# Gate/up products of the feed-forwards: 19 of 22 pieces as seven block products of half the tokens, modulation products moved behind them

## What is computed

```python
for l in range(DEPTH_2):            # 2
    mod = (c_act @ w_mod[l] + b_mod[l]).reshape(c.shape[0], N_MOD, D_MODEL)
    h = modulate(x, g_norm[l, 0], mod[:, 0], mod[:, 1])
    x = x + 0.5 * mod[:, 2][:, None, :] * swiglu_2(h, w_ffn1_gu[l], w_ffn1_down[l])
    ...
    h = modulate(x, g_norm[l, 2], mod[:, 6], mod[:, 7])
    x = x + 0.5 * mod[:, 8][:, None, :] * swiglu_2(h, w_ffn2_gu[l], w_ffn2_down[l])

def modulate(x, g, shift, scale):
    return rmsnorm_2(x, g) * (1.0 + scale[:, None, :]) + shift[:, None, :]
```

## Time and profile before

| | us |
|---|---|
| median of 3 runs | 3005.95 |
| lowest, highest | 3005.54, 3012.29 |
| span of the profiled execution | 2999.2 |
| TensorE busy in it | 2885.2 |
| VectorE, ScalarE, POOL busy in it | 1808.9, 1307.9, 326.0 |

### The profile page before, as it was taken

The page is one execution under the profiler, slowest core; times in us unless marked ns, Lnnn a source line. Parts: engine busy times, 40 slices in busy tenths (PEclk is TensorE's granted clock), DMA queues, the critical chain, the costliest instruction groups (busy, mean ns, idle before and its releaser), DMA issues. The chain is left out here.

```text
span 2999.2 us, 39355 instructions
## 1 busy us (share of the span) xinstructions
PE 2885.2 (96%) x13800; PEld 2294.2 (76%) x13800; DVE 1808.9 (60%) x2177; ACT 1307.9 (44%) x1512; POOL 326.0 (11%) x425
## 2 busy tenths in 40 slices
PE   8999798999999999999999999999999999999998
PEld 4876566777777778888877788887888877788886
DVE  7747857999999987555158555425554156533323
ACT  5125535888888863233136322213322136332312
POOL 0100012333333320000000000000000000000000
PEclk9989999999999999999999999999999999999999
DMA  8552236999999996553222255423554222122221
GB/s 320 169 197 92 100 152 247 370 361 372 373 365 355 367 367 237 192 188 134 98 102 71 94 200 195 154 95 106 193 194 154 98 96 77 65 104 98 97 87 68
DMA packets 115843, 555.50 MB, mean 185 GB/s; under 512 B 20656, under 2 KB 22192, under 8 KB 73776
## 3 DMA queue, kind: packets, MB, share of 16 engines
q1 hardware_dynamic: 89264, 491.43, 44.3%
q0 software_dynamic: 26496, 62.96, 5.9%
HBM read 549.10 MB, written 37.75 MB: 196 GB/s over the span
## 5 line engine op out<-in xcount | busy, mean ns | idle before, releaser
L168 ACT ACTIVATE stream_high<-stream_raw 128x2048 fp32r<-128x2048 f32 x151 | 289.3, 1917 | 799.8 <-PE ffn_ps_psum L470 755.0
L173 DVE TENSOR_TENSOR stream_low<-stream_raw,stream_high 128x2048 fp32r<-128x2048 f32 x156 | 356.7, 2287 | 406.9 <-ACT stream_high L168 406.5
L468 PE MATMUL ffn_ps_psum<-h_high_f,stream_high 128*128 128x512 f32 x1344 | 523.3, 389 | 0.2 <-DVE stream_low L173 0.2
L470 PE MATMUL ffn_ps_psum<-h_high_f,stream_low 128*128 128x512 f32 x1344 | 522.8, 389 | 0.0
L469 PE MATMUL ffn_ps_psum<-h_low_f,stream_high 128*128 128x512 f32 x1344 | 522.8, 389 | 0.0
L312 DVE TENSOR_TENSOR expert_low<-expert_raw,expert_high 128x2048 fp32r<-128x2048 f32 x128 | 292.8, 2288 | 6.1 <-ACT expert_high L308 2.5
L692 DVE TENSOR_TENSOR ffn_sg<-ffn_sg,ffn_ps_psum 128x512 f32<-128x512 f32 x88 | 60.5, 687 | 388.5 <-PE ffn_ps_psum L470 385.6
L468 PEld LDWEIGHTS ffn_ps_psum<-h_high_f,stream_high 128*128 128x128 f32 x1344 | 252.3, 188 | 53.5 <-DVE stream_low L173 0.6
L469 PEld LDWEIGHTS ffn_ps_psum<-h_low_f,stream_high 128*128 128x128 f32 x1344 | 252.3, 188 | 52.8 <-issue 0.2
L470 PEld LDWEIGHTS ffn_ps_psum<-h_high_f,stream_low 128*128 128x128 f32 x1344 | 252.3, 188 | 51.8
L468 PE MATMUL ffn_ps_psum<-ffn_hid_high,stream_high 128*128 (+1 forms) x704 | 277.6, 394 | 3.2 <-DVE ffn_sg L692 3.2
(11 more groups left out here) (497 smaller groups left out, 5050.7 us busy)
## 6 DMA issues: line engine op xcount, KB each, us to landing
expert_raw<-in_exp_gu SPq DMA_DIRECT2D x128, 1024.0 KB
stream_raw<-in_ffn_gu SPq DMA_DIRECT2D x88, 1024.0 KB, 5.0
expert_raw<-in_exp_dn SPq DMA_DIRECT2D x64, 1024.0 KB
con<-in_w_mod SPq DMA_DIRECT2D x120, 512.0 KB
stream_raw<-in_ffn_dn SPq DMA_DIRECT2D x44, 1024.0 KB, 5.0
mix_mod_rows<-in_w_ada POOLq DMA_DIRECT2D x32, 512.0 KB
stream_raw<-in_w_in SPq DMA_DIRECT2D x16, 1024.0 KB, 5.0
pieces_raw<-in_w_in SPq DMA_DIRECT2D x11, 1024.0 KB, 6.9
```

Of the source, the lines that this page charges most:

```text
L168: self.nc.scalar.activation(self.high[:, q], self.raw[:, q], ACT.Copy).then_inc(self.high_done, 1)
L173: self.nc.vector.tensor_tensor(self.low[:, q], self.raw[:, q], self.high[:, q].bitcast(F32), ALU.subtract)\
L468: mm(out, w[0], x[0], start=start, stop=False)
L470: return mm(out, w[1], x[0], start=False, stop=stop)
```

## The change

**Products.** Pieces 0 to 2 of the up phase stay as they were (`PLAIN` = 3). For pieces 3 to 21 the gate and up weights are one 2 by 2 matrix of blocks: gate or up, times the first or last four of the 8 width blocks (the host stores the four quarters one behind the other, `PLACE`). The tokens are 2 by 2 too: first or last four width blocks, times the first or last 256 tokens. Two by two block matrices can be multiplied with seven block products in place of eight (Winograd's form of Strassen's), from sums of blocks on both sides and sums of the products. A product is 4 width blocks × 3 matmuls of 256 columns, so a piece is 84 matmuls of 256 columns, where it was 48 of 512.

**Sums of the tokens**, once per feed-forward: the normed tokens in 32 bits on ScalarE (8 Identity), 4 sums of 1024 on VectorE, and high and low parts of them (`t_high`, `t_low`).

**Sums of the weights**, for each of the 19 pieces: products one, two and four take three quarters of the weights as they are, whose high part (1536 columns) ScalarE puts in `pure_high` and whose low part VectorE puts in `pure_low`. Then VectorE makes four sums of 512 columns in place in `stream_raw`, each of the last three waiting for the one before, and the split of before (2048 columns, ScalarE then VectorE) is made of those sums, for the products six, seven, five and three. ScalarE's waits for all four sums.

**Sums of the products.** ScalarE keeps product one and five (256 columns each), VectorE adds: first rows (2 × 256), middle rows (512), last rows (512 and 256); ScalarE makes silu of the gate, VectorE the product of gate and up into `hid`, in 32 bits. The parts of `hid` are no longer made per piece: POOL makes the high part of two tiles (`window`) and VectorE the low part, per piece of the down phase, in the space of the pure blocks.

**Moved.** The modulation rounds stand in the down phase, 4 products per piece, behind the split and the window; their loads stand between the down loads on SP. The late norm's squares go to ScalarE's turns of pieces 8 to 11, its sums to POOL, its 8 products to rounds 1 and 2 of the down phase. Its sum is TensorE's after piece 12, in bank 7.

The diff, cut to its core:

```diff
+PLAIN = 3
+LATE = 8
+PLACE = {(0, 0): 0, (0, 1): 1, (1, 1): 2, (1, 0): 3}
...
+plain_banks = [(0, 1), (6, 7), (0, 1)]
+half_bank = lambda s, i: ps[:, 6, TOK[s]] if i == two else ps[:, 3 * s + i // 2, TOK[i % 2]]
...
+        in_pairs(sp, FT, up, first=1)
+        down(0, 0)
+        down(0, 1)
         if beside:
-            def beside_up(g):
-                up(2 * g + 1, 0)
-                mod.load(sp, g, (0, 1))
-                up(2 * g + 1, 1)
-                mod.load(sp, g, (2, 3))
-                up(2 * g + 2, 0)
-                mod.load(sp, g, (4, 5))
-                up(2 * g + 2, 1)
+            def round_(g):
+                down(g + 1, 0)
+                mod.load(sp, g, (2, 3, 4, 5))
+                down(g + 1, 1)
                 mod.load(sp, g, (6, 7))
-            with sp.Fori(0, rounds) as g:
-                beside_up(g)
-        in_pairs(sp, FT, up, first=1 + 2 * rounds)
-        in_pairs(sp, HALF, down)
+                mod.load(sp, g + 1, (0, 1))
+            mod.load(sp, 0, (0, 1))
+            with sp.Fori(0, rounds - 1) as g:
+                round_(g)
+            down(rounds, 0)
+            mod.load(sp, rounds - 1, (2, 3, 4, 5, 6, 7))
...
+        def product(out, weights, place, x, tok, rows_=0, start=True, stop=True):
+
+            for k in range(4):
+                c = slice(place * S + k * P, place * S + (k + 1) * P)
+                mm = mm3(out, (weights[0][:, c], weights[1][:, c]), (x[0][:, rows_ + k, tok], x[1][:, rows_ + k, tok]),
+                         start=start and k == 0, stop=stop and k == 3)
+            return mm
+
+        def seven_products(r, s):
+            n = 2 * r + s
+            m = number(n)
+            pure, sums, t_ = (pure_h[:, s], pure_l[:, s]), (w.high[:, w.slot(s)], w.low[:, w.slot(s)]), (t_high, t_low)
+            tok0, tok1 = TOK
+            out = lambda i: half_bank(s, i)
+            pe.wait_ge(pure_low, m + 1)
+            pe.wait_ge(hid_done, n - 1)
+            product(out(one), pure, 0, h, tok0).then_inc(products, 1)
+            if not (isinstance(m, int) and m < 1):
+                pe.wait_ge(rows_made, 4 * m - 2)
+            product(out(two), pure, 1, h, tok0, 4).then_inc(products, 1)
+            if isinstance(n, int) and n == PLAIN:
+                pe.wait_ge(t_ready, 2)
+            product(out(four), pure, 2, t_, tok0, 4).then_inc(products, 1)
+            w.ready(pe, r, s)
+            pe.wait_ge(kept, 2 * m + 1)
+            product(out(six), sums, 0, t_, tok1, 4).then_inc(products, 1)
+            product(out(seventh), sums, 3, t_, tok1, 0).then_inc(products, 1)
+            product(out(five), sums, 2, t_, tok0, 0).then_inc(products, 1)
+            product(out(three), sums, 1, h, tok1, 4).then_inc(w.used, 1)
...
+        def silus(r, s):
+            m = number(2 * r + s)
+            act.wait_ge(rows_made, 4 * m + 4)
+            a(rows[s][:, 0:2, :], rows[s][:, 0:2, :], ACT.Silu).then_inc(silu_done, 1)
+
+        def keep_first(r, s):
+            m = number(2 * r + s)
+            act.wait_ge(products, 6 * m + 1)
+            if not (isinstance(m, int) and m < 2):
+                act.wait_ge(hid_done, 2 * r + (s - 1))
+            a(rows[s][:, 0, :], half_bank(s, one), ACT.Copy).then_inc(kept, 1)
+
+        def keep_fifth(r, s):
+            act.wait_ge(products, 6 * number(2 * r + s) + 6)
+            a(fifth[s], half_bank(s, five), ACT.Copy).then_inc(kept, 1)
+
+        def split_pure(r, s):
+            m = number(2 * r + s)
+            wait_loaded(act, r, s)
+            if not (isinstance(m, int) and m < 2):
+                act.wait_ge(products, 6 * m - 9)
+            a(pure_h[:, s], w.raw[:, w.slot(s), 0:3 * S], ACT.Copy).then_inc(pure_high, 1)
+
+        def split_sums(r, s):
             n = 2 * r + s
-            act.wait_ge(gate_ps, n + 1)
-            act.wait_ge(hid_low_done, n + 1)
-            nc.scalar.activation(sg[:, s, :], ps[:, 2 * s, :], ACT.Silu).then_inc(silu_done, 1)
+            act.wait_ge(sums_made, 4 * number(n) + 4)
+            act.wait_ge(w.used, n + (w.base - 1))
+            a(w.high[:, w.slot(s)], w.raw[:, w.slot(s)], ACT.Copy).then_inc(w.high_done, 1)
...
+        def body(r, s, silu=None, pure=True):
+            before = (r, 0) if s else (r - 1, 1)
+            behind = (r, 1) if s == 0 else (r + 1, 0)
+            (silu or silus)(*before)
+            keep_first(r, s)
+            split_sums(*behind)
+            keep_fifth(r, s)
+            if pure:
+                split_pure(r + 1, s)
...
+        def window(r, s):
+            n = 2 * r + s
+            pool.wait_ge(hid_done, 4 * r + 2 * s + 2)
+            if isinstance(n, int) and n < 2:
+                pool.wait_ge(products, 6 * number(FT - 2 + n) + 3)
+            else:
+                pool.wait_ge(w.used, n + (w.base + FT - 1))
...
+        def split_pure(r, s):
+            m = number(2 * r + s)
+            dve.wait_ge(pure_high, m + 1)
+            v.tensor_tensor(pure_l[:, s], w.raw[:, w.slot(s), 0:3 * S], pure_h[:, s].bitcast(F32), ALU.subtract).then_inc(pure_low, 1)
+        def make_sums(r, s):
+            m = number(2 * r + s)
+            a11, a12, a22, a21 = (w.raw[:, w.slot(s), i * S:(i + 1) * S] for i in range(4))
+            dve.wait_ge(pure_low, m + 1)
+            for i, (out, x, y, op) in enumerate(((a22, a21, a22, ALU.add), (a21, a11, a21, ALU.subtract),
+                                                 (a11, a22, a11, ALU.subtract), (a12, a12, a11, ALU.subtract))):
+                if i:
+                    dve.wait_ge(sums_made, 4 * m + i)
+                v.tensor_tensor(out, x, y, op).then_inc(sums_made, 1)
+        def first_rows(r, s):
+            m = number(2 * r + s)
+            q, made = rows[s], rows_made
+            dve.wait_ge(kept, 2 * m + 1)
+            dve.wait_ge(products, 6 * m + 4)
+            v.tensor_tensor(q[:, 2, :], q[:, 0, :], half_bank(s, six), ALU.add).then_inc(made, 1)
+            dve.wait_ge(made, 4 * m + 1)
+            v.tensor_tensor(q[:, 0, :], q[:, 0, :], half_bank(s, two), ALU.add).then_inc(made, 1)
+        def middle_rows(r, s):
+            m = number(2 * r + s)
+            q = rows[s]
+            dve.wait_ge(kept, 2 * m + 2)
+            v.tensor_tensor(q[:, 1:4:2, :], q[:, 2, :].unsqueeze(1).broadcast_to([P, 2, S // 2]), both_halves(s, five), ALU.add)\
+                .then_inc(rows_made, 1)
+        def last_rows(r, s):
+            n = 2 * r + s
+            q = rows[s]
+            dve.wait_ge(w.used, n + (w.base + 1))
+            dve.wait_ge(rows_made, 4 * number(n) + 3)
+            v.tensor_tensor(q[:, 1:3, :], q[:, 1:4:2, :], both_halves(s, three), ALU.add).then_inc(rows_made, 1)
+            dve.wait_ge(kept, 2 * number(n) + 2)
+            dve.wait_ge(rows_made, 4 * number(n) + 4)
+            v.tensor_tensor(q[:, 3, :], q[:, 3, :], fifth[s], ALU.add).then_inc(last_row, 1)
...
+            v.tensor_tensor(hid_tile(n).rearrange("p (a t) -> p a t", a=2), rows[s][:, 0:2, :], rows[s][:, 2:4, :], mult)\
+                .then_inc(hid_done, 1)
...
+        low, high = TOK
+        dve.wait_ge(t_base, 4)
+        v.tensor_tensor(first_k[:, :, low], first_k[:, :, high], first_k[:, :, low], ALU.subtract).then_inc(t_made, 1)
...
+        def body(r, s, before=None):
+            behind = (r, 1) if s == 0 else (r + 1, 0)
+            (before or last_rows)(*((r, 0) if s else (r - 1, 1)))
+            split_pure(*behind)
+            if not before:
+                finish(*((r, 0) if s else (r - 1, 1)))
+            make_sums(*behind)
+            first_rows(r, s)
+            w.split_low(dve, *behind)
+            middle_rows(r, s)
...
+            def round_(g):
+                down(g, 0)
+                if late and g in (1, 2):
+                    late_norm(4 * g - 4)
+                    late_norm(4 * g - 3)
+                mod.multiply(dve, g, (0, 1, 2, 3))
+                down(g, 1)
+                if late and g in (1, 2):
+                    late_norm(4 * g - 2)
+                    late_norm(4 * g - 1)
+                mod.multiply(dve, g, (4, 5, 6, 7))
                 mod.finish(dve, g)
...
```

348 lines of the change are left out of this document (222 added, 126 removed).

## The result

The changed kernel takes 3094.39 us (median of 4, 3084.16 to 3095.46), the kernel before on the same chips 3007.09 (3005.54 to 3012.29): a ratio of 1.028, interval 1.0262 to 1.0298. It is slower by 2.8%, where 3043 was forecast; 3094 lies at the upper edge of the range of 2990 to 3095. The profiled execution has a span of 3082.3 us, 83.1 more than before.

A forecast was written before the change was run, and what follows sets the result against it. TensorE alone was taken to bound the kernel before, VectorE's chain with ScalarE the changed one. Up phases +12, down phases +20, late norm +8, first down piece −3 make +37 on 3005.95: 3043 us, range 2990 to 3095.

The forecast's parts named there:

- The bound: Up phase: TensorE alone sets the pace before; after, the VectorE and ScalarE chain is 1.15 us longer than TensorE needs.
- the hole: Up phase, each piece: VectorE idle some 1.2 us while ScalarE makes the high part of the four sums.
- TensorE's piece: Up phase: 84 matmuls of 256 columns at 0.1205 us make 10.12 us, 0.76 under the 10.88 before.
- The turn: Up phase: VectorE's loop with ScalarE's step takes 11.27 us per piece; +3 us per feed-forward, +12 in four.
- the wait at the first down piece: Start of the down phase: TensorE's wait of 0.78 us goes in all four feed-forwards, −3 us.
- The down phase: Three feed-forwards with modulation: VectorE's piece takes 11.25 us against TensorE's 10.88; +6.5 us three times, +20.
- The tail: End of the down phase: last product ends after 116 us, next weights queue behind modulation loads, adds start at 120.2.
- The late norm: First network's eight operations, moved into down-phase rounds 1 and 2: 5.4 us plus some 2.5 for the logarithm, +8.
- the later expectation: For the kernel before with modulation moved: VectorE's piece 10.7 us, below TensorE's 10.88; the window's 1.15 then tips it over.
- B: Rival, up phase: VectorE's wait for its own semaphore costs nothing, turn 10.60 us, kernel 2991 us; chance 0.22.
- C: Rival, down phase: modulation loads land sooner, in 3.5 us; VectorE's piece 10.7, −12 in all, 3031 us; chance 0.15.
- D: Rival: a 256-column matmul takes over 0.134 us, TensorE is the bound again; 3098 us at 0.140; chance 0.12.

The follow-up runs named there:

- the halves: Changed kernel with ScalarE's high part of a piece's sums, and VectorE's low part, made in two halves of 1024 columns: 3013.79 us, ratio 1.0028.
- four slots: Changed kernel with four slots in place of two for the modulation's loads in the down phase: 3016.24 us, ratio 1.0033.

## Why the prediction was right or wrong, point by point

**The bound.** Right: the turn of VectorE and ScalarE replaces TensorE as what sets the up phase's pace, and the halves show it by taking the hole away.

**TensorE's piece.** 0.1205 us per matmul was forecast between bounds of 0.1115 and 0.127; it is 0.120 (1864.11 to 1864.23). The rival in which these matmuls take over 0.134 falls, though a weight load's record still lasts longer than that.

**The turn.** 11.27 forecast, 11.18 to 11.19 measured. The dependent adds cost 0.13 each, where the sum had 0.14 (its two rows give 0.15); the hole is 1.28 where 1.2 stood; TensorE's pause is ahead of the fourth product and is released by ScalarE's keeping of the first, as said. It shows 0.85 idle and not 1.1; the first matmul behind it, at 0.22 to the next in place of 0.12 (1855.38 to 1855.60 in the piece before), is a part of what is missing. The four up phases give +12 (248.3 + 244.8 + 243.4 + 244.8 less 969.6), where +12 for the turn and −3 for the wait at the first down piece stood.

**The down phase** is the step that failed, in its size. I had +20 for three and +8 for the late norm; it is +71. The mechanism is the one named: the third product of a piece waits for a load that is issued only when a slot comes free, and VectorE's piece is longer than TensorE's. What was mis-sized is that piece: 11.25 us stood, and a round of two pieces takes 25.1 us (107.3 less 6.7, in four) and not 22.5. Over the pieces of the second and third feed-forward the means are:

| step of a piece on VectorE | forecast | measured |
|---|---|---|
| first product to third | 5.46 | 5.96 |
| third to fourth | 1.15 | 1.61 |
| fourth to the next piece's first | 4.65 | 4.88 |

In the first step, 0.3 is the load: from its issue to its product 4.05 stood, and 4.37 is the mean. The rest of that step is the first product, 1.43 in the mean where 1.22 stood, as it can last up to 2.06 beside GpSimd's cast. In the second step the fourth product waits for its own load, issued 1.2 us after the third's and landing later still; the sum had no such wait. In the third step, the round's sum L137 with the loop's turn costs 0.7 that I had at 0.15. The piece shown above has 5.97 and 1.44. The load of its third product was issued at 2006.7, beside the fourth's and the weights':

```profile
DMA to landing us min/median/max: 4.5/4.5/4.5
```

and of all loads of this line, of which 120 are the modulation's in the three feed-forwards (3.3 to 6.1) and the others are earlier ones issued by GpSimd:

```profile
DMA to landing us min/median/max: 3.3/4.3/7.7
```

Of the second and third feed-forward's loads, the first and fifth of a round, issued with the least beside them, land in 3.4 to 4.1 us; the others in 3.5 to 6.1, most in 4.2 to 4.7. Weights land late too, 6.5 us in the median where it was 5.0:

```profile
stream_raw<-in_ffn_dn SPq DMA_DIRECT2D x44, 1024.0 KB, 6.5
```

The 2.6 us per round have no cushion to fall on, as 22.5 was over TensorE's 21.75 already, so all of it goes to the end: the last product ends 127.5 us into the phase and not 116.

The 4.05 was also a weak reading. It came from one load, whose 4.33 less the 0.20 between the two engines' issues is 4.13 and not 4.05, and whose time was below the median of its group: 4.6, which less the same 0.20 is 4.4, close to the 4.37 measured here. It was not read on a quiet queue either; the kernel before moved as much per us in that stretch as the changed kernel does in its first down phase (DMA share 0.64, 218 GB/s):

```profile
66.00:70.40 4.40, 4.40 (x21) 3.65 (x20) 1.29 (x3) 0.60 (x1) 1.06 (x2) 1.00 0.64 218
```

**The tail.** Adds were to start at 120.2 and start at 133.1 in feed-forwards 2 and 3: 11.5 from the products, 1.4 from the next weights, whose load is queued behind the last modulation load, as said. With the other order on SyncE's queue that wait is gone, but the products end later. Then comes a cost that was not in the sum at all: after 9.3 us of idle time TensorE's matmuls are 0.43 apart for a while, 1.2 GHz in place of 2.4, and as VectorE's adds wait for them (3.40 us at 2127.41), the last add of the second feed-forward ends at 145.9, another 2.4 later. In the first and third it is 1.9 and 1.3.

**The late norm.** +8 forecast beyond the others; the first feed-forward's down phase is 27.5 longer, the others' 22.1 and 21.0, so +6, and its up phase is 2 to 3 longer than those of the others. About right.

**The window** was thought to be what tips VectorE over TensorE's pace only by the later expectation, and the kernel before with its modulation moved shows that it is not needed for that.

**The rivals.** The free wait (B) is refuted by the sums 0.73 apart and by the run in which they don't wait. Loads landing sooner (C) was the wrong side of the latency. Of D only the time came true, by another mechanism.

## What to carry to other kernels

When work is moved out of one engine's idle time, its loads move too. With two slots a load can be issued only when a product has ended, so part of each latency stands in the chain; idle time hides it and a busy chain does not. Take that latency from the median of a group of loads and not from one row, count the wait of every load and not of the first alone, and if the sum is within a few per cent of the next engine's pace, take the long end, as everything over it arrives at the end of the phase.

When two engines pass a piece back and forth, add their times in order and look for what stands beside each hand-over; here halving the handed piece was worth 80 us by the medians and more slots 78 (71 and 72 by the traces), each nearly what the whole change had cost, and only with both was the kernel faster than before.

## What the runs showed of the hardware that I had not expected

**GpSimd beside VectorE.** A cast of 128x1024 on GpSimd and a VectorE operation with two inputs in SBUF, the memory that both read, stretch each other. Timelines of POOL and of VectorE in the changed kernel:

```profile
2041.48 2.04 POOL L805 CAST ffn_pure_high<-ffn_hid 128x1024 fp32r x1 [9.72 <-PE ffn_ps_psum L475]
```

```profile
2041.40 1.22 DVE L892 TENSOR_TENSOR ffn_pure_low<-ffn_hid,ffn_pure_high 128x1024 fp32r<-128x1024 f32 x1
2042.54 2.06 DVE L131 SCALAR_TENSOR_TENSOR con<-con,c_row 128x1024 f32<-128x1024 f32 x1
```

Alone they take 1.04 and 1.22. The cast's end, 43.52, is 0.9 after L892's end at 42.62, and L131's end, 44.60, is 1.08 after the cast's: as if one ran after the other. The Trainium skill ("SBUF — State Buffer", "SBUF: two separate sides") says so, an exclusive lock held for the whole instruction; the rows agree.

**Loads beside each other.** Of the modulation's loads (512 KB), those issued with the least beside them mostly land in 3.4 to 3.7 us, the others mostly in 4.2 to 4.7. The down phase's weights (1 MB) land in 4.7 to 5.1 us with no other load beside them and in 6.1 to 9.0 beside the modulation's.

**The clock after an idle stretch.** In the three tails, 9.3 us of idle TensorE in the second feed-forward among them, the slow matmuls cost a further 1.3 to 2.4 us. The first two down phases of the changed kernel show a granted clock of 0.92 and 0.95, the first one without pauses (four slots) 1.00. Most of what is missing lies in the tail: in the second feed-forward the clock is 0.60 from 2116 to 2123 us, where TensorE idles, and 0.54 from 2123 to 2128.
